# Earlier weight splits, an earlier statistics start and an earlier residual at the LayerNorm seams of a two-layer decoder kernel

## The chip, the cores and the metric

The kernel runs on one core of one Trainium2 chip. The metric is the device time of one execution in microseconds (us). The kernel before took 1182.99 us (median of 3 runs, 1182.77 to 1183.74).

The core's engines run side by side and meet at semaphores: PE is TensorE (matmuls), DVE is VectorE, ACT is ScalarE, POOL is GpSimd, SP issues the loads. Each engine takes its own instructions strictly in the order in which they are written; an instruction that waits holds up everything behind it on its engine.

## The reference

One step of a two-layer decoder over 512 prompt tokens and 32 sample tokens (8 sequences of 4), model width 1024, MLP width 4096, all in float32. What matters here is the shape of the chain:

```
for i in range(2):
    if i == 0:  m = recurrent_mixer(x, ...)        # Griffin block, ends in  (h * y) @ w_out + b_out
    else:       m = sliding_window_attention(x)    # x @ w_qkv ..., softmax with sink, @ w_o + b_o
    x = layer_norm(ALPHA * x + m, ln1_g[i], ln1_b[i])
    x = layer_norm(ALPHA * x + square(relu(x @ w_up[i])) @ w_down[i], ln2_g[i], ln2_b[i])

def layer_norm(x, g, b):
    mu = mean(x); var = mean(square(x - mu))
    return (x - mu) * rsqrt(var + 1e-5) * g + b
```

There are four LayerNorms, numbered L = 0 to 3 in the code: L = 0 and 2 follow a mixer's output projection, L = 1 and 3 follow an MLP. The whole token batch goes through all of them.

## The kernel before

**Layout.** The model dimension lies on the 128 partitions in eight tiles (k or m = 0 to 7), tokens lie on the free axis. The 544 tokens are two halves: h = 0 has 256, h = 1 has 288. `acc` holds the running sum, `x_hi` and `x_lo` the current activations.

**Two-part numbers.** Each float32 operand of a matmul is split in a high part (rounded) and a low part (the rest), and a product is three matmuls: hi\*hi, lo\*hi, hi\*lo. So each weight slab (128x1024) is loaded to one of 4 `stage` buffers, copied by ACT to `w_hi` (line 476) and subtracted by DVE to `w_lo` (line 797). This pair of operations is called a split of a slab. There are 8 slab slots; ACT's part of a split waits until the matmuls that last used the slot are done. The load of slab j waits for the DVE part of slab j-4.

**A seam.** Between a projection or MLP (PE) and the next one lies a LayerNorm, done half by half, so that the statistics of one half run beside the matmuls of the other. For each tile of the projection, DVE adds the PSUM bank to `acc` (line 969) and `acc` to a running sum (line 976): `add_tile`. ACT squares the tile (`square`, line 595; two `sqt` buffers, so the square of tile m waits for POOL's work on tile m-2), and POOL adds the squares up (`add_square`, line 1254). After tile 7, PE turns the two sums into a mean and a mean square for every partition with two matmuls against ones (`norm_sums`, lines 1375 and 1378); ACT copies the mean (603), DVE makes the variance (984 to 987), ACT takes the root (605), DVE subtracts the mean (1011), inverts the root (1014) and multiplies (1017), ACT writes `x_hi` and the scaled `acc` (616, 617; two tiles make a pair), DVE writes `x_lo` for the pair (1006, called the low step).

**Where norm_sums stands on PE.** For half 1 it stands inside the next group of matmuls (`group_by_half`, lines 1410 to 1412): after k = 1 in the first `up` group of an MLP, after k = 3 in the first q/k/v group. PE is in order, so the rest of the group is behind it.

**Work inside the seams.** The engines' idle places are filled by hand: `norm_apply` takes callbacks. In `tiles` (seams L = 0 and L = 2), `beside(t)` runs once for each pair t of half 0 and deals with the tiles of half 1 and with the first four slabs of the MLP (`late`). In `mlp`, the steps `up(l, 0)` to `up(l, 3)` (ACT: relu at 651, square at 653; DVE: square at 1053, low part at 1057) and the splits of slabs j0+4 to j0+7 (which the first `down` product reads, lines 1498 to 1500) lie between the LayerNorm's steps of half 1.

**POOL's residual.** For L = 1, POOL multiplies the normalised `acc` by ALPHA and adds the next bias (`residual`, line 1265), eight tiles a half; each waits for the low step of its pair. For l = 0 it stands behind all additions of squares of half 1.

The three places that the change touches are called seam A (L = 0 and the start of the first MLP, 170 to 215 us), seam C (L = 1, from the first MLP to q/k/v, 565 to 610 us) and seam E (L = 2 and the start of the second MLP, 757 to 802 us, the same code as A).

Of the kernel before, what the change touches and what calls it, by code (L numbers as in the profile page):

```python
# [73 lines left out]
def build(nc, xp_t, xs_t, vec, w_y, w_x, w_ga, w_gi, w_out, w_qkv, w_o, w_up, w_down,  # L74
          ck_t, cache_k, cache_v, y_t, small, k_p, v_p, k_s, v_s):
    ctx = ExitStack()
    with ctx:
# [374 lines left out]
        def _(act):  # L452
# [135 lines left out]
            def square(L, h, m):  # L588

                c0, n = HALF[h]  # L590
                pos = tile_pos(L, h, m)
                act.wait_ge(s_evV, read_by(unit_of("down" if L % 2 else "o", L, h, m) + 1, "V"))
                if pos >= 2:
                    act.wait_ge(s_s2, pos - 1)
                A(sqt[:, pos % 2, :n], acc[:, m, c0:c0 + n], ACT.Square).then_inc(s_sqt, 1)

            def norm_stats(L, h):
                _, n = HALF[h]
                m0 = mark[("ln", L, h)]
                idx = 2 * L + h  # L600
                if idx:
                    act.wait_ge(s_xhat, 4 * idx)
                A(mean[:, :n], unit(m0)[:, :n], ACT.Copy).then_inc(s_evA, 1)
                act.wait_ge(s_var, idx + 1)
                A(rstd[:, :n], msq[:, :n], ACT.Sqrt).then_inc(s_std, 1)
# [17 lines left out]
            def tiles(L, early, late):  # L623


                def beside(t):
                    if t:
                        square(L, 1, 2 + t)
                        split(late[t - 1:t])

                for m in range(KT):
                    split(early[m:m + 1])
                    square(L, 0, m)
                square(L, 1, 0)
                norm_stats(L, 0)
                square(L, 1, 1)
                square(L, 1, 2)
                norm_apply(L, 0, beside)
                square(L, 1, 6)
                square(L, 1, 7)  # L640
                split(late[3:])

            def up(l, q, c=0, i=0):

# [10 lines left out]
            def mlp(l):  # L655
                j0 = job_at[("mlp", l)][0]
                j7 = j0 + 8 * (CHUNKS - 1)
                L = 2 * l + 1
                norm_stats(2 * l, 1)
                split(range(j0 + 4, j0 + 6))  # L660
                up(l, 0)
                up(l, 1)
                split([j0 + 6])
                up(l, 2)
                split([j0 + 7])
                up(l, 3)
                norm_apply(2 * l, 1)
                for q in range(4, 8):
                    up(l, q)
                split(range(j0 + 8, j0 + 12))  # L670
                with act.Fori(0, CHUNKS - 2) as i:
                    for q in range(4):
                        for k in ((0, 1), (2,), (3,), ())[q]:
                            split([j0 + 12 + k], i, 8, 24, down_unit(l, 0, 1, 7) + 1)
                        up(l, q, 1, i)
                    for q in range(4, 8):
                        up(l, q, 1, i)

                    split(range(j0 + 16, j0 + 20), i, 8, 24, up_unit(l, 1, 1, 3) + 1)
                for q in range(4):  # L680
                    for k in ((0, 1), (2,), (3,), ())[q]:
                        split([j7 + 4 + k])
                    up(l, q, CHUNKS - 1)
                for m in range(KT):
                    square(L, 0, m)
                up(l, 4, CHUNKS - 1)
                norm_stats(L, 0)
                up(l, 5, CHUNKS - 1)
                up(l, 6, CHUNKS - 1)

                def beside(t):
                    if t == 1:
                        up(l, 7, CHUNKS - 1)
                    if t >= 2:
                        square(L, 1, 2 * t - 4)
                        square(L, 1, 2 * t - 3)

                norm_apply(L, 0, beside)
                gj = job_at[("qkv", 0)][0]
                for m in range(4, KT):  # L700
                    if l == 0:
                        split([gj + m - 4])
                    square(L, 1, m)

            tiles(0, (), next_slabs(("mlp", 0)))
            mlp(0)
# [75 lines left out]
        def _(dve):  # L782
# [240 lines left out]
            def add_tile(name, L, h, m):  # L1023
                n0 = unit_of(name, L, h, m)
                tile_done(L, h, m, unit(n0), read_by(n0 + 1, "V"))

            def tiles(name, L, early, late):


                def beside(t):  # L1030
                    add_tile(name, L, 1, 3 + t)
                    if t:
                        split(late[t - 1:t])

                for m in range(KT):
                    add_tile(name, L, 0, m)
                    if m % 2:
                        split(early[m // 2:m // 2 + 1])
                add_tile(name, L, 1, 0)
                norm_stats(L, 0)  # L1040
                norm_apply(L, 0, beside, after_centre=lambda: add_tile(name, L, 1, 1),
                           after_root=lambda: add_tile(name, L, 1, 2))
                add_tile(name, L, 1, 7)
                split(late[3:])

            def up(l, q, c=0, i=0):

# [25 lines left out]
            def mlp(l):  # L1073
                j0 = job_at[("mlp", l)][0]
                j7 = j0 + 8 * (CHUNKS - 1)
                L = 2 * l + 1
                norm_stats(2 * l, 1)

                def rest():
                    for q in range(1, 4):  # L1080
                        up(l, q)
                        if q > 1:
                            split([j0 + 4 + q])

                def sums(t):
                    if t == 1 or t == 2:
                        accumulate(l, 0, 0, 2 * t - 2)
                        accumulate(l, 0, 0, 2 * t - 1)

                norm_apply(2 * l, 1, sums, after_centre=lambda: (split([j0 + 4, j0 + 5]), up(l, 0)), after_root=rest)  # L1090
                for m in range(4, KT):
                    accumulate(l, 0, 0, m)
                for q in range(4, 8):
                    up(l, q)
                for m in range(KT):
                    if m < 4:
                        split([j0 + 8 + m])
                    accumulate(l, 0, 1, m)
                with dve.Fori(0, CHUNKS - 2) as i:
                    for q in range(4):  # L1100
                        for k in ((0, 1), (2,), (3,), ())[q]:
                            split([j0 + 12 + k], i, 8)
                        up(l, q, 1, i)
                    for m in range(KT):
                        accumulate(l, 1, 0, m, i)
                    for q in range(4, 8):
                        up(l, q, 1, i)
                    for m in range(KT):
                        if m < 4:
                            split([j0 + 16 + m], i, 8)  # L1110
                        accumulate(l, 1, 1, m, i)
                for q in range(4):
                    for k in ((0, 1), (2,), (3,), ())[q]:
                        split([j7 + 4 + k])
                    up(l, q, CHUNKS - 1)
                for m in range(KT):
                    add_tile("down", L, 0, m)
                up(l, 4, CHUNKS - 1)
                norm_stats(L, 0)
                gj = job_at[("qkv", 0)][0]  # L1120

                def ups(t):
                    if t == 0:
                        up(l, 6, CHUNKS - 1)

                def tail(t):
                    if t == 0:
                        up(l, 7, CHUNKS - 1)
                    if t == 1 or t == 2:
                        add_tile("down", L, 1, 2 * t - 2)  # L1130
                        add_tile("down", L, 1, 2 * t - 1)

                norm_apply(L, 0, tail, ups,
                           after_centre=lambda: up(l, 5, CHUNKS - 1))
                for m in range(4, KT):
                    add_tile("down", L, 1, m)
                    if l == 0:
                        split([gj + m - 4])

            dve.wait_ge(s_res0, 2)  # L1140
            tiles("o", 0, (), next_slabs(("mlp", 0)))
# [67 lines left out]
        def _(pool):  # L1209
# [65 lines left out]
            def mlp(l):  # L1275
                L = 2 * l + 1
                for m in range(KT):
                    add_square(L, 0, m)
                if l:
                    residual(L, 0)  # L1280
                for m in range(KT):
                    add_square(L, 1, m)
                if l == 0:
                    residual(L, 0)
                residual(L, 1)

            tiles(0)
# [461 lines left out]
```

## Time and profile before

| | |
|---|---|
| median of 3 runs | 1182.99 us |
| the profiled execution: own time | 1182.99 us |
| the profiled execution: span of the trace | 1181.2 us |
| PE busy | 1125.2 us (95%) |
| DVE busy | 686.8 us (58%) |
| ACT busy | 522.3 us (44%) |
| POOL busy | 166.1 us (14%) |
| mean granted clock of TensorE | 0.978 |

The page gives busy time by engine; the list of waits says for whom PE stood idle; the timeline gives every instruction with its start, its duration and, in square brackets, the idle time of its engine before it and what ended it. A row with x4 merges four instructions. Starts are counted from the beginning of the span.

### The profile page before, as it was taken

What the parts mean: (1) busy time and instruction counts of PE and PEld (TensorE: products, weight loads), DVE (VectorE), ACT (ScalarE), POOL (GpSimd) and SP (SyncE); (2) the same over time, 40 slices, a digit from 0 to 9 for tenths busy, and PEclk for the clock granted to TensorE, in tenths of its full rate; (3) what the DMA queues carried; (4) which work ended last, traced back from release to release, by engine and by line L of the source; (5) the groups of instructions that cost most, each with busy time, mean ns of one, the idle gap of its engine ahead of it and who ended that gap; (6) DMA issues with size and microseconds to landing.
All of it is one profiled execution on the core that took longest, in us unless ns stands there. A gap on an engine that the chain in (4) does not pass through costs nothing.

```text
span 1181.2 us, 23125 instructions
## 1 busy us (share of the span) xinstructions
PE 1125.2 (95%) x8783; PEld 1098.9 (93%) x8783; DVE 686.8 (58%) x1277; ACT 522.3 (44%) x1009; POOL 166.1 (14%) x205
## 2 busy tenths in 40 slices
PE   7899899999999999999999789999999999999994
PEld 7899899999999999999989458999999999999994
DVE  6888788545354463546942981685453543535566
ACT  5899836424232242233644991463242232422333
POOL 3212131000100000002530771210000000000024
PEclk9899899999999999999999898999999999999997
DMA  8222304133241230422311120042240422403202
GB/s 256 82 80 90 125 2 129 52 108 111 107 142 59 83 128 16 140 71 72 88 56 42 54 73 19 1 143 71 73 137 16 131 71 71 142 19 123 72 4 73
DMA packets 51468, 98.42 MB, mean 83 GB/s; under 512 B 4448, under 2 KB 20256, under 8 KB 51392
## 3 DMA queue, kind: packets, MB, share of 16 engines
q1 hardware_dynamic: 50720, 94.81, 25.2%
q0 software_dynamic: 400, 2.21, 0.5%
q8 instruction: 39, 0.64, 0.2%
q10 hardware_dynamic: 288, 0.59, 0.1%
q14 instruction: 21, 0.17, 0.0%
HBM read 95.06 MB, written 3.56 MB: 83 GB/s over the span
## 4 chain that ended last, share of the span: by engine, by line
PE 77%; DVE 10%; ACT 7%; issue 2%; POOL 2%; DMA 1%; SPq 0%; POOLq 0%; DVEq 0%; ACTq 0%
PE bank L1332 18%; PE bank L1333 18%; PE bank L1334 18%; PE bank L1500 5%; PE bank L1498 5%; PE bank L1499 5%; DVE w_lo L797 2%; PE bank L1410 1%; PE bank L1412 1%; PE bank L1411 1%; ACT w_hi L476 1%; POOL w_lo L1309 1%; DVE acc L1011 1%; DVE xc_odd L927 1%; PE bank L1580 1%
## 5 line engine op out<-in xcount | busy, mean ns | idle before, releaser
L1332 PE MATMUL bank<-x_hi,w_hi 128*128 128x288 f32 (+1 forms) x1360 | 397.2, 292 | 7.9 <-DVE w_lo L797 7.9
L1333 PE MATMUL bank<-x_lo,w_hi 128*128 128x288 f32 (+1 forms) x1360 | 395.3, 291 | 0.0
L1334 PE MATMUL bank<-x_hi,w_lo 128*128 128x288 f32 (+1 forms) x1360 | 393.2, 289 | 0.0
L1332 PEld LDWEIGHTS bank<-x_hi,w_hi 128*128 128x128 f32 x1360 | 259.2, 191 | 9.2 <-DVE w_lo L797 8.6
L1334 PEld LDWEIGHTS bank<-x_hi,w_lo 128*128 128x128 f32 x1360 | 259.7, 191 | 0.0
L1333 PEld LDWEIGHTS bank<-x_lo,w_hi 128*128 128x128 f32 x1360 | 259.4, 191 | 0.1
L797 DVE TENSOR_TENSOR w_lo<-stage,w_hi 128x1024 fp32r<-128x1024 f32 x162 | 198.1, 1236 | 45.5 <-ACT w_hi L476 45.5
L476 ACT ACTIVATE w_hi<-stage 128x1024 fp32r<-128x1024 f32 x170 | 172.3, 1049 | 117.2 <-PE bank L1334 112.3
L651 ACT ACTIVATE relu<-bank 128x256 f32<-128x256 f32 (+1 forms) x128 | 50.9, 398 | 352.4 <-PE bank L1334 329.1
L1333 PE MATMUL bank<-m_lo,w_hi 128*128 128x288 f32 (+1 forms) x608 | 176.0, 289 | 0.0
L1332 PE MATMUL bank<-m_hi,w_hi 128*128 128x288 f32 (+1 forms) x608 | 175.4, 289 | 0.0
L1334 PE MATMUL bank<-m_hi,w_lo 128*128 128x288 f32 (+1 forms) x608 | 175.2, 288 | 0.0
L1053 DVE TENSOR_TENSOR h_sq<-relu 128x256 f32<-128x256 f32 (+1 forms) x128 | 56.6, 442 | 172.0 <-ACT relu L651 172.0
L1070 DVE TENSOR_TENSOR acc<-bank,acc 128x256 f32<-128x256 f32 (+1 forms) x192 | 79.7, 439 | 129.8 <-PE bank L1334 65.5
L1498 PE MATMUL bank<-m_hi,w_hi 128*128 128x288 f32 (+1 forms) x512 | 148.1, 289 | 1.6 <-DVE w_lo L797 1.5
L1500 PE MATMUL bank<-m_hi,w_lo 128*128 128x288 f32 (+1 forms) x512 | 147.7, 288 | 0.0
L1499 PE MATMUL bank<-m_lo,w_hi 128*128 128x288 f32 (+1 forms) x512 | 147.4, 288 | 0.0
L1332 PEld LDWEIGHTS bank<-m_hi,w_hi 128*128 128x128 f32 x608 | 114.7, 189 | 0.0
L1333 PEld LDWEIGHTS bank<-m_lo,w_hi 128*128 128x128 f32 x608 | 114.5, 188 | 0.0
L1334 PEld LDWEIGHTS bank<-m_hi,w_lo 128*128 128x128 f32 x608 | 114.3, 188 | 0.0
L1498 PEld LDWEIGHTS bank<-m_hi,w_hi 128*128 128x128 f32 x512 | 96.5, 188 | 2.7 <-issue 2.2
L1499 PEld LDWEIGHTS bank<-m_lo,w_hi 128*128 128x128 f32 x512 | 96.5, 188 | 0.0
(188 smaller groups left out, 1522.2 us busy)
## 6 DMA issues: line engine op xcount, KB each, us to landing
stage<-w_up SPq DMA_DIRECT2D x64, 512.0 KB, 4.0
stage<-w_down SPq DMA_DIRECT2D x64, 512.0 KB, 3.6
stage<-w_qkv SPq DMA_DIRECT2D x10, 512.0 KB, 4.4
stage<-w_x SPq DMA_DIRECT2D x8, 512.0 KB, 5.0
stage<-w_y SPq DMA_DIRECT2D x8, 512.0 KB, 4.4
stage<-w_out SPq DMA_DIRECT2D x8, 512.0 KB, 4.1
stage<-w_o SPq DMA_DIRECT2D x8, 512.0 KB, 3.8
y_t<-acc SPq DMA_DIRECT2D x8, 144.0 KB, 1.9
```

Of the source, the lines that this page charges most:

```text
L476: A(hi, raw, ACT.Copy).then_inc(s_whi, 1)
L651: A(relu[:, q % 2, :n], bank[:, n0 % BANKS, :n], ACT.Relu).then_inc(s_evA, 1)
L797: vt.tensor_tensor(lo, raw, hi.bitcast(F32), ALU.subtract).then_inc(s_wlo, 1)
L927: ins = vt.scalar_tensor_tensor(xp, u[:, t, k:k + 256], wk, xp, ALU.mult, ALU.add)
L1053: vt.tensor_tensor(h_sq[:, q % 2, :n], relu[:, q % 2, :n], relu[:, q % 2, :n], ALU.mult)\
L1070: ins = vt.tensor_tensor(a, bank[:, n0 % BANKS, :n], a, ALU.add)
L1332: mm(out, wh, xh, start=(k == 0), stop=False)
L1333: mm(out, wh, xl, start=False, stop=False)
L1334: ins = mm(out, wl, xh, start=False, stop=(k == last))
L1498: mm(out, wh, xh, start=(k == 0), stop=False)
L1499: mm(out, wh, xl, start=False, stop=False)
L1500: ins = mm(out, wl, xh, start=False, stop=(k == 3))
```

## The change

Four edits, none of which changes what is computed.

1. In `tiles` (A, E): `beside(t)` deals with half 1's tile 3+t on both engines and splits slab `late[t]`. Before, ACT squared tile 2+t, neither engine split at t = 0, and the last slab came after tile 7.
2. At the start of `mlp` (A, E): the splits of slabs j0+4 and j0+5 move ahead of `norm_stats`, that of j0+6 to the place behind the centring, that of j0+7 between `up(l, 2)` and `up(l, 3)`; on DVE, `up(l, 2)` and `up(l, 3)` come after the first of the four multiplications.
3. At the end of the first MLP (C): the splits of the q/k/v slabs start at tile 6 instead of tile 4, so two of the four come after tile 7.
4. On POOL (C): `residual(1, 0)` goes ahead of half 1's additions of squares.

```
 ACT, tiles:    def beside(t):
-                    if t:
-                        square(L, 1, 2 + t)
-                        split(late[t - 1:t])
+                    square(L, 1, 3 + t)
+                    split(late[t:t + 1])
...
                 norm_apply(L, 0, beside)
-                square(L, 1, 6)
                 square(L, 1, 7)
-                split(late[3:])
 ACT, mlp:
+                split(range(j0 + 4, j0 + 6))
                 norm_stats(2 * l, 1)
-                split(range(j0 + 4, j0 + 6))
-                up(l, 0)
-                up(l, 1)
-                split([j0 + 6])
-                up(l, 2)
-                split([j0 + 7])
-                up(l, 3)
+                split(range(j0 + 6, j0 + 8))
+                for q in range(4):
+                    up(l, q)
...
                 for m in range(4, KT):
-                    if l == 0:
-                        split([gj + m - 4])
+                    if l == 0 and m >= 6:
+                        split([gj + m - 6])
                     square(L, 1, m)
+                if l == 0:
+                    split([gj + 2, gj + 3])
 DVE, tiles:
                     add_tile(name, L, 1, 3 + t)
-                    if t:
-                        split(late[t - 1:t])
+                    split(late[t:t + 1])
...
-                norm_apply(2 * l, 1, sums, after_centre=lambda: (split([j0 + 4, j0 + 5]), up(l, 0)), after_root=rest)
+                norm_apply(2 * l, 1, sums, ups, after_centre=lambda: (split([j0 + 6]), up(l, 0)),
+                           after_root=lambda: up(l, 1))
...
 POOL, mlp:
-                if l:
-                    residual(L, 0)
+                residual(L, 0)
                 for m in range(KT):
                     add_square(L, 1, m)
-                if l == 0:
-                    residual(L, 0)
                 residual(L, 1)
```

**ACT in seam A, before,** from pair 0 of half 0 (four rows of 616 and 617) to the square of tile 3 and the end of pair 1. Line numbers are those of the kernel named.

```order
L616 ACTIVATE x_hi<-acc,vecs 128x256
L617 ACTIVATE acc<-acc,vecs 128x256
L616 ACTIVATE x_hi<-acc,vecs 128x256
L617 ACTIVATE acc<-acc,vecs 128x256
L616 ACTIVATE x_hi<-acc,vecs 128x256
L617 ACTIVATE acc<-acc,vecs 128x256
L616 ACTIVATE x_hi<-acc,vecs 128x256
L617 ACTIVATE acc<-acc,vecs 128x256
L595 ACTIVATE sqt<-acc 128x288
L476 ACTIVATE w_hi<-stage 128x1024
```

The same place in the changed kernel:

```order
L616 ACTIVATE x_hi<-acc,vecs 128x256
L617 ACTIVATE acc<-acc,vecs 128x256
L616 ACTIVATE x_hi<-acc,vecs 128x256
L617 ACTIVATE acc<-acc,vecs 128x256
L595 ACTIVATE sqt<-acc 128x288
L476 ACTIVATE w_hi<-stage 128x1024
L616 ACTIVATE x_hi<-acc,vecs 128x256
L617 ACTIVATE acc<-acc,vecs 128x256
L616 ACTIVATE x_hi<-acc,vecs 128x256
L617 ACTIVATE acc<-acc,vecs 128x256
```

The square of tile 3 and the first slab's copy now stand after pair 0 instead of after pair 1.

**DVE in seam A, before,** at pairs 0 and 1 of half 0: the low step (1006), then the two additions of one tile of half 1 (969, 976), then from pair 1 on a slab's low part (797).

```order
L1006 TENSOR_TENSOR x_lo<-acc,x_hi 128x2x256
L969 TENSOR_TENSOR acc<-bank,acc 128x288
L976 TENSOR_TENSOR sum_b<-acc,sum_b 128x288
L1006 TENSOR_TENSOR x_lo<-acc,x_hi 128x2x256
L969 TENSOR_TENSOR acc<-bank,acc 128x288
L976 TENSOR_TENSOR sum_b<-acc,sum_b 128x288
L797 TENSOR_TENSOR w_lo<-stage,w_hi 128x1024
```

The same place in the changed kernel:

```order
L1002 TENSOR_TENSOR x_lo<-acc,x_hi 128x2x256
L965 TENSOR_TENSOR acc<-bank,acc 128x288
L972 TENSOR_TENSOR sum_b<-acc,sum_b 128x288
L793 TENSOR_TENSOR w_lo<-stage,w_hi 128x1024
L1002 TENSOR_TENSOR x_lo<-acc,x_hi 128x2x256
L965 TENSOR_TENSOR acc<-bank,acc 128x288
L972 TENSOR_TENSOR sum_b<-acc,sum_b 128x288
L793 TENSOR_TENSOR w_lo<-stage,w_hi 128x1024
```

On DVE the additions keep their place behind the low step; only a slab's low part is added at pair 0.

**POOL in seam C,** before: the additions of squares of half 0 (`sumsq_a`) and half 1 (`sumsq_b`), then the residual of half 0 (128x256) and half 1.

```order
L1254 TENSOR_TENSOR sumsq_a<-sqt,zeros 128x256
L1254 TENSOR_TENSOR sumsq_a<-sqt,sumsq_a 128x256 x7
L1254 TENSOR_TENSOR sumsq_b<-sqt,zeros 128x288
L1254 TENSOR_TENSOR sumsq_b<-sqt,sumsq_b 128x288 x7
L1265 TENSOR_SCALAR acc<-acc,vecs 128x256 x8
L1265 TENSOR_SCALAR acc<-acc,vecs 128x288 x8
```

And in the changed kernel:

```order
L1252 TENSOR_TENSOR sumsq_a<-sqt,zeros 128x256
L1252 TENSOR_TENSOR sumsq_a<-sqt,sumsq_a 128x256 x7
L1263 TENSOR_SCALAR acc<-acc,vecs 128x256 x8
L1252 TENSOR_TENSOR sumsq_b<-sqt,zeros 128x288
L1252 TENSOR_TENSOR sumsq_b<-sqt,sumsq_b 128x288 x7
L1263 TENSOR_SCALAR acc<-acc,vecs 128x288 x8
```

The eight residual steps of half 0, each of which waits for a low step, now stand ahead of every addition of half 1's squares.

## Rows read from the trace of the kernel before

**Rows 1.** List of waits of PE: line, whom it waited for, us in total, times, longest.

```profile
PE bank L1410 <- DVE acc L1068: 2.7, 2, 1.4
```

**Rows 2.** Timeline of PE, seams A and E: start, duration, line, operation, idle before.

```profile
189.35 0.65 PE L1375 MATMUL bank<-sum_b,ones 128*128 128x288 f32 x2
189.83 0.65 PE L1378 MATMUL bank<-sumsq_b,ones 128*128 128x288 f32 x2
...
204.64 0.36 PE L1498 MATMUL bank<-m_hi,w_hi 128*128 128x256 f32 x1 [0.34 <-DVE w_lo L797]
...
213.33 0.37 PE L1410 MATMUL bank<-x_hi,w_hi 128*128 128x288 f32 x1 [1.37 <-DVE acc L1068]
...
776.27 0.65 PE L1375 MATMUL bank<-sum_b,ones 128*128 128x288 f32 x2
```

**Rows 3.** Timeline of ACT, seam A: squares, slab copies and a pair's first write.

```profile
176.85 0.43 ACT L595 ACTIVATE sqt<-acc 128x288 f32<-128x288 f32 x1
177.18 1.04 ACT L476 ACTIVATE w_hi<-stage 128x1024 fp32r<-128x1024 f32 x1
178.13 0.59 ACT L616 ACTIVATE x_hi<-acc,vecs 128x256 fp32r<-128x256 f32 x1
...
180.10 0.43 ACT L595 ACTIVATE sqt<-acc 128x288 f32<-128x288 f32 x1
```

**Rows 4.** Timeline of DVE, seam A: low steps, additions, statistics, a hidden low part, multiplications.

```profile
175.80 0.45 DVE L969 TENSOR_TENSOR acc<-bank,acc 128x288 f32<-128x288 f32 x1
176.28 0.46 DVE L976 TENSOR_TENSOR sum_b<-acc,sum_b 128x288 f32<-128x288 f32 x1
...
180.30 0.69 DVE L1006 TENSOR_TENSOR x_lo<-acc,x_hi 128x512 fp32r<-128x512 f32 x1 [0.43 <-ACT acc L617]
...
190.54 0.46 DVE L984 TENSOR_TENSOR msq<-mean 128x288 f32<-128x288 f32 x1 [0.70 <-ACT mean L603]
...
202.94 0.43 DVE L1057 TENSOR_TENSOR m_lo<-h_sq,m_hi 128x256 fp32r<-128x256 f32 x1
...
204.41 2.76 DVE L1017 TENSOR_TENSOR acc<-acc,rstd 128x576 f32<-128x576 f32 x4
```

**Rows 5.** Timeline of POOL: seam A's last addition, seam C's residuals of both halves.

```profile
187.70 0.82 POOL L1254 TENSOR_TENSOR sumsq_b<-sqt,sumsq_b 128x288 f32<-128x288 f32 x1 [0.67 <-ACT sqt L595]
...
585.95 10.12 POOL L1265 TENSOR_SCALAR acc<-acc,vecs 128x256 f32<-128x256 f32 x8
601.10 0.99 POOL L1265 TENSOR_SCALAR acc<-acc,vecs 128x288 f32<-128x288 f32 x2 [5.03 <-DVE x_lo L1006]
```

**Rows 6.** Timeline of ACT, seam C: the first q/k/v slab and the fifth.

```profile
575.29 1.04 ACT L476 ACTIVATE w_hi<-stage 128x1024 fp32r<-128x1024 f32 x1
...
585.14 1.06 ACT L476 ACTIVATE w_hi<-stage 128x1024 fp32r<-128x1024 f32 x1 [0.17 <-DMA stage<-w_qkv]
```

**Rows 7.** Timeline of DVE, seam C: the last low step, the first slab, statistics, two slabs.

```profile
575.65 1.30 DVE L1006 TENSOR_TENSOR x_lo<-acc,x_hi 128x512 fp32r<-128x512 f32 x1
...
577.73 1.22 DVE L797 TENSOR_TENSOR w_lo<-stage,w_hi 128x1024 fp32r<-128x1024 f32 x1
...
588.10 0.65 DVE L984 TENSOR_TENSOR msq<-mean 128x288 f32<-128x288 f32 x1
...
592.71 2.55 DVE L797 TENSOR_TENSOR w_lo<-stage,w_hi 128x1024 fp32r<-128x1024 f32 x2
```

**Rows 8.** Timeline of PE, seam C: starts of the three q/k/v groups.

```profile
579.68 0.35 PE L1410 MATMUL bank<-x_hi,w_hi 128*128 128x256 f32 x1 [1.80 <-DVE acc L969]
...
595.31 0.39 PE L1332 MATMUL bank<-x_hi,w_hi 128*128 128x256 f32 x1 [2.84 <-DVE w_lo L797]
...
608.33 0.29 PE L1410 MATMUL bank<-x_hi,w_hi 128*128 128x288 f32 x1
```

**Rows 9.** Loads of the page: operation, count, size, us to landing.

```profile
stage<-w_qkv SPq DMA_DIRECT2D x10, 512.0 KB, 4.4
```

**Rows 10.** Stretches: busy us of PE, PEld, DVE, ACT, POOL, granted clock, DMA, GB/s.

```profile
596.00:598.00 2.00, 2.00 (x11) 2.00 (x11) 1.97 (x3) 0.05 (x1) 0.07 (x1) 0.50 0.89 286
```

More of the change, by code:

```diff
@@ L1043, in tiles @@
                 add_tile(name, L, 1, 7)
-                split(late[3:])
             def up(l, q, c=0, i=0):
@@ L1076, in mlp, with ups @@
                 L = 2 * l + 1
+                split(range(j0 + 4, j0 + 6))
                 norm_stats(2 * l, 1)
[L1079 to L1083, printed above, removed]
+                def ups(t):
+                    if t == 0:
+                        up(l, 2)
+                        split([j0 + 7])
+                        up(l, 3)
                 def sums(t):
@@ L1135, in mlp @@
                 for m in range(4, KT):
+                    if l == 0 and m >= 6:
+                        split([gj + m - 6])
                     add_tile("down", L, 1, m)
-                    if l == 0:
-                        split([gj + m - 4])
+                if l == 0:
+                    split([gj + 2, gj + 3])
             dve.wait_ge(s_res0, 2)
@@ L1278, in mlp @@
                     add_square(L, 0, m)
-                if l:
-                    residual(L, 0)
+                residual(L, 0)
                 for m in range(KT):
                     add_square(L, 1, m)
-                if l == 0:
-                    residual(L, 0)
                 residual(L, 1)
```

## The prediction

> **What bounds the kernel now.** PE is busy for 1125 of 1181 us, so the time is PE's matmuls plus the places where PE stands. The list of waits comes first: away from the beginning and the attention part it shows three stops at the LayerNorm seams. Twice 1.4 us before an `up` group that waits for DVE to free its banks [rows 1], once 1.80 and once 2.84 us in seam C [rows 8]. The timeline of PE says what stands ahead of each stop. In seams A and E the statistics matmuls run at 189.35 and 776.27 without a wait [rows 2]; the two seams are the same code, 586.92 us apart, so I work out A and count it twice. Outside the seams PE never stands between 214 and 549 us, nor in the second MLP, so a delay of PE at the end of a seam is carried in full to the end of the kernel. The timelines of ACT, DVE and POOL then say which engine feeds the statistics, and how much room it has.
>
> **Edit 1, seams A and E: the pairs of half 0.** Before, ACT's step for one pair is: four writes, one square, one slab copy. Squares start at 176.85 and 180.10, a period of 3.25 us [rows 3]: ACT's own work, with no idle time, because the tile that ACT squares after pair t was added by DVE after pair t-1. Now ACT squares tile 3+t right behind pair t, and DVE adds that tile only behind its low step of the same pair, which in turn waits for ACT's last write of that pair. So one step is a serial chain over both engines:
>
> - pair's first write to DVE's low step: 178.13 to 180.30, 2.17 us [rows 3, 4]
> - low step to addition: 180.30 to 180.91, 0.61; the addition itself 0.45 [rows 4]
> - square to slab copy 0.33, slab copy to the next pair's first write 0.95 [rows 3]
>
> Sum 4.51 us, against 3.25. The first tile's addition (tile 3) stands at 175.80, done 176.25 [rows 4], so pair 1 starts at 176.25 + 0.33 + 0.95 = 177.53, pair 2 at 182.04, pair 3 at 186.55. Tile 6 is added at 186.55 + 2.78 = 189.33; the last slab's copy runs from 190.11 to 191.15; DVE's low part of it (1.22 us by the row in seam C [rows 7], 1.14 to the next start) until 192.3; only then tile 7 is added, until 192.75, squared by 193.2, and POOL's 0.82 us [rows 5] ends at 194.1. The second statistics matmul, which PE issued at 189.83 [rows 2], can start at about 194.2. PE is in order, so it stands from 189.35 to 194.2 but for one matmul: a new stop of 4.4 us beyond the old time. The banks don't bring it forward: the tiles that the `up` group overwrites are added by about 185.4.
>
> **Edit 2, seams A and E: the start of the MLP.** After square 7 ACT copies slabs j0+4 and j0+5 (193.1 to 195.1; their loads have landed, since their buffers come free earlier than before), DVE makes their low parts until 196.4, and the variance starts there: 5.9 us later than 190.54 [rows 4]. From here the new order is better. Before, the low part of `up(l, 3)` was done at 203.37, 12.83 us after the variance's start [rows 4]. Of the three slab parts that lay between, two are left (-1.14), and one multiplication is added (2.76 / 4 = +0.69 [rows 4]): 12.4 us, so 208.8. PE's `down` product needs that part for k = 3; from its k = 3 to the end of the product PE took from 204.64 to 213.33 - 1.37 = 211.96, 7.32 us [rows 2], or 0.122 a matmul for 60. The product so ends at 216.2. The 1.37 us stop for the banks goes: the first multiplication is done early, so ACT writes pair 0 while DVE is still in the `up` steps, and the four banks are free at about 215.5, which is 0.7 us too early to count. Net for A: 216.2 - 213.33 = +2.9 us.
>
> To this comes the clock. With the full clock PE would have 1.5 us to spare before 208.9 (194.4 + 72 x 0.12 + 36 x 0.12 = 207.4). The stop of 2.84 us before 595.31 [rows 8] was followed by a granted clock of 0.50 [rows 10], the 1.2 GHz level, and the q/k/v group behind it took 608.33 - 595.31 = 13.02 us for 96 matmuls, 1.5 us more than 96 x 0.12. One such spell fits in the spare 1.5 us and costs nothing; two cost about 1.7. Bounds for A: +1.2 (DVE never late, PE's own work alone: 194.4 + 168 x 0.12 = 214.6) and +4.6 (two spells). I take +3.4, near the chain with a little of the clock; E the same.
>
> The Trainium skill, "TensorE: Matmul & The Clock Gate", Part 1, says that an array left idle falls to half rate and must be busy again before it is let up. By that rule each new stop of almost 5 us surely brings a slow spell; by the row alone it is likely. The rule would move each of A and E towards its upper bound.
>
> **Edits 3 and 4, seam C.** ACT's square of tile m waits for POOL's addition of tile m-2. Before, POOL was idle there. Now eight residual steps stand ahead of its first addition, and the last two wait for the low step of pair 3, which ended at 576.95 [rows 7]. A residual step costs 0.50 us alone and 10.12 / 8 = 1.27 beside a busy DVE [rows 5], so POOL reaches tile 0 at about 578 and ends it at 579. ACT's square of tile 2 waits for it, and squares 3, 4, 5 follow at POOL's pace, 0.85 to 0.9 each: 582. Edit 3 has put the first q/k/v slab behind square 5; its copy began at 575.29 [rows 6], now at about 582.1. With 1.04 for the copy and 1.22 for the low part PE can start q/k/v at 584.4 instead of 579.68 [rows 8]: +4.7 us. Bounds: 583.3 with every POOL step at its undisturbed price, 586.5 with every one at 1.27 or more.
>
> Then the next slabs are late too. DVE is done with the second one at about 586.4 (tile 6 stands between), its buffer's load takes 4.4 us [rows 9], and copy and low part 2.3: 593.2. The variance starts there instead of at 588.10 [rows 7]. Its steps and the centring took 592.71 - 588.10 = 4.6 us beside POOL's residuals; these are gone, so 4.0. Two slabs more, 2.4 instead of 2.55 [rows 7]: the group at 595.31 starts at 599.6, +4.3. PE will by then have finished the group before at about 599, so it hardly stands a second time, and the 1.5 us of slow clock behind 595.31 are not paid here. Group q/k/v of half 1 starts at 599.6 + 11.5 = 611.1 instead of 608.33 [rows 8]: +2.8. I take +2.7. Bounds: +0.5 (undisturbed POOL, no slow spell) and +6 (two slow spells, loads at twice the wait).
>
> The Trainium skill, "SBUF — State Buffer", "Who interferes with whom", says that a DVE instruction with two SBUF inputs and a GpSimd instruction that reads SBUF block each other. The rows agree (0.50 against 1.27). This rule speaks for edit 4, but what it could give back is the 0.6 us that I took at the variance.
>
> **Sum.** 3.4 + 2.7 + 3.4 = 9.5 us. The profiled execution took 1182.99 us (span 1181.2 and 1.8 around it), which is the median of the runs too. Forecast 1192.5.
>
> **Rivals.**
>
> 1. Two slow spells of the clock at each new stop. For it: three stops of about 5 to 6 us each. Against: in A and E a part lies under DVE's chain. Price: A and E 4.6, C 5.0: 1197.2. Chance 0.17.
> 2. Seam C costs next to nothing: POOL catches up and the second stop's slow spell is saved. For it: POOL's low price alone [rows 5]. Price: C +0.5, A and E at the chain's 2.9: 1189.3. Chance 0.18.
> 3. Not slower: tile 7's sums reach PE by about 189.8, the stop never arises, and the bank stop (1.37) and the stop of 0.34 ahead of 204.64 [rows 2] go. From the start of pair 1 the chain needs two steps and 7.5 us, so this needs a step of 2.4 us or less where 4.5 is worked out; it could only be if DVE didn't queue the additions behind the low steps. Price: 2 x -1.7, C 0: 1179.6. Chance 0.04.
> 4. The change trades evenly: shorter chains after the variance give back what the stops take. PE's own work sets +1.2 in A as a floor, so this needs seam C to gain 2.4. 1183.0, chance 0.03.
>
> **How the numbers follow.** My own case has 0.58. Changes under 0.2% (2.4 us) can't be told from none. Range 1187.5 to 1197.5: it covers rivals 1 and 2 and both bounds but the outermost. Faster 0.04, same 0.03, slower 0.93.
>
> **What would show it.** In the changed profile PE waits for `sum_b` or `sumsq_b` at the statistics matmuls of A and E, 4 to 5 us each; ACT's squares in A stand 4.5 us apart and wait for DVE's addition; the two bank waits are gone; in C ACT's square of tile 2 waits for POOL, and the first q/k/v group waits 6 to 7 us for a slab's low part. If squares in A stay 3.25 apart, or no wait stands at the statistics matmuls, I am wrong.

## The result and the profile after

The changed kernel takes 1191.23 us (median of 4 runs, 1190.14 to 1192.63), against 1182.88 us for the kernel before in the same comparison: ratio 1.0073, 95% interval 1.0055 to 1.0090. It is slower by about 8.5 us. The profiled execution has a span of 1188.6 us (1181.2 before); about 1 us of the difference to the medians is that this execution reached seam A 0.95 us earlier, at 185.54 instead of 186.49. The lead is there before anything that the edits moved: the first write of pair 0, at 171.94 instead of 172.89, is as much earlier. Across all runs below that start lies between 185.5 and 187.4. So I compare stretches, from PE's first matmul of one group to that of another, and not only whole times.

From the list of waits of PE in the changed kernel (line, whom it waited for, us in total, times, longest):

```profile
PE bank L1370 <- DVE sum_b L972: 9.1, 3, 4.0
...
PE bank L1327 <- DVE w_lo L793: 6.3, 4, 3.3
PE bank L1405 <- DVE w_lo L793: 5.2, 1, 5.2
```

The two bank waits of [rows 1] are gone. In their place stand two waits of 4.0 us at the statistics matmuls (the third, of 1.0, stands at the end of the kernel in both) and one of 5.2 at the first q/k/v group. The timeline of PE in seams A and E, to be read against [rows 2]:

```profile
192.56 1.33 PE L1370 MATMUL bank<-sum_b,ones 128*128 128x288 f32 x2 [4.01 <-DVE sum_b L972]
193.69 1.17 PE L1373 MATMUL bank<-sumsq_b,ones 128*128 128x288 f32 x2
194.24 0.83 PE L1405 MATMUL bank<-x_hi,w_hi 128*128 128x256 f32 x1
...
204.66 0.28 PE L1493 MATMUL bank<-m_hi,w_hi 128*128 128x256 f32 x1
...
216.07 0.29 PE L1405 MATMUL bank<-x_hi,w_hi 128*128 128x288 f32 x1
...
784.96 1.33 PE L1370 MATMUL bank<-sum_b,ones 128*128 128x288 f32 x2 [4.01 <-DVE sum_b L972]
```

The pairs of half 0 on ACT ([rows 3] before). Each square now waits 1.2 to 1.3 us for DVE's addition of the same tile:

```profile
175.32 0.45 ACT L595 ACTIVATE sqt<-acc 128x288 f32<-128x288 f32 x1 [1.30 <-DVE acc L965]
175.67 1.05 ACT L476 ACTIVATE w_hi<-stage 128x1024 fp32r<-128x1024 f32 x1
176.62 0.58 ACT L616 ACTIVATE x_hi<-acc,vecs 128x256 fp32r<-128x256 f32 x1
...
179.88 0.45 ACT L595 ACTIVATE sqt<-acc 128x288 f32<-128x288 f32 x1 [1.20 <-DVE acc L965]
```

And on DVE ([rows 4] before), where the addition follows the low step, which waits for ACT's last write; then the variance and the end of `up(l, 3)`:

```profile
178.79 0.69 DVE L1002 TENSOR_TENSOR x_lo<-acc,x_hi 128x512 fp32r<-128x512 f32 x1 [0.81 <-ACT acc L617]
179.40 0.45 DVE L965 TENSOR_TENSOR acc<-bank,acc 128x288 f32<-128x288 f32 x1
...
195.75 0.45 DVE L980 TENSOR_TENSOR msq<-mean 128x288 f32<-128x288 f32 x1
...
207.90 0.42 DVE L1051 TENSOR_TENSOR m_lo<-h_sq,m_hi 128x256 fp32r<-128x256 f32 x1
```

Seam C, the starts of the three q/k/v groups on PE ([rows 8] before):

```profile
585.79 0.55 PE L1405 MATMUL bank<-x_hi,w_hi 128*128 128x256 f32 x1 [5.24 <-DVE w_lo L793]
...
601.25 0.39 PE L1327 MATMUL bank<-x_hi,w_hi 128*128 128x256 f32 x1 [0.83 <-DVE w_lo L793]
...
612.75 0.29 PE L1405 MATMUL bank<-x_hi,w_hi 128*128 128x288 f32 x1
```

The stretches of all runs, in us. A and E run from the first `up` matmul of half 0 to the first `up` matmul of half 1. C runs from the start of the last `down` product of half 1; the three columns are the starts of the first q/k/v group, the second, and the first one of half 1. The medians come from several comparisons, in which the kernel before had 1182.18 to 1183.06; each ratio is to the kernel before of its own comparison and isn't simply the quotient of the medians shown.

| run | A | E | C: first | C: second | C: half 1 | median | ratio and interval |
|---|---|---|---|---|---|---|---|
| before | 26.84 | 26.83 | 14.72 | 30.35 | 43.37 | 1182.88 (with the changed kernel) | |
| changed | 30.53 | 29.81 | 18.16 | 33.62 | 45.12 | 1191.23 | 1.0073 (1.0055 to 1.0090) |
| ae_only (edits 1, 2) | 30.49 | 29.89 | 14.73 | 30.34 | 41.86 | 1187.67 | 1.0052 (1.0037 to 1.0066) |
| c_only (edits 3, 4) | 26.86 | 26.87 | 18.17 | 33.98 | 45.50 | 1183.70 | 1.0012 (1.0003 to 1.0021) |
| edit1_only | 32.24 | 31.68 | 14.73 | 30.34 | 43.31 | 1192.59 | 1.0088 (1.0074 to 1.0102) |
| edit2_only | 25.17 | 25.16 | 14.72 | 30.34 | 41.86 | 1177.28 | 0.9960 (0.9947 to 0.9974) |
| square_lag | 24.89 | 24.90 | 14.72 | 30.34 | 41.85 | 1177.32 | 0.9960 (0.9946 to 0.9974) |
| add_ahead | 25.35 | 25.69 | 14.72 | 30.36 | 43.40 | 1178.64 | 0.9966 (0.9954 to 0.9978) |
| edit3_only | 26.85 | 26.87 | 16.16 | 32.97 | 45.91 | 1185.70 | 1.0029 (1.0018 to 1.0040) |
| edit4_only | 26.86 | 26.87 | 16.76 | 31.55 | 43.07 | 1181.69 | 0.9996 (0.9987 to 1.0005) |
| edit3_add_first | 26.84 | 26.84 | 16.37 | 31.66 | 43.07 | 1182.87 | 1.0001 (0.9991 to 1.0011) |
| residual_last | 26.85 | 26.84 | 14.72 | 29.42 | 42.38 | 1180.46 | 0.9983 (0.9974 to 0.9992) |
| edit2_residual_last | 25.16 | 25.17 | 14.73 | 29.50 | 41.02 | 1177.23 | 0.9954 (0.9940 to 0.9968) |
| lag_residual_last | 24.91 | 24.90 | 14.72 | 29.52 | 41.03 | 1175.62 | 0.9940 (0.9926 to 0.9953) |

The changed kernel's span follows from its row: A +3.69, C +1.75, E +2.98, and -0.95 ahead of A make +7.5; the spans differ by 7.4. The stretches between the seams agree with before to 0.1 us.

### The profile page after: what moved, and what is told of

The parts are those of the page before. It is cut to its first block, busy times and chain, and to the rows that moved or that the text cites. A ratio compares the mean times of both kernels' runs of the same rounds, so it can differ in the third digit from the quotient of the medians.

```text
span 1188.6 us, 23125 instructions
## 1 busy us (share of the span) xinstructions
PE 1128.6 (95%) x8783; PEld 1101.3 (93%) x8783; DVE 683.7 (58%) x1277; ACT 522.7 (44%) x1009; POOL 153.3 (13%) x205
## 4 chain that ended last, share of the span: by engine, by line
PE 80%; DVE 8%; ACT 6%; POOL 2%; issue 2%; DMA 1%; SPq 0%; POOLq 0%; DVEq 0%; ACTq 0%
PE bank L1327 18%; PE bank L1328 18%; PE bank L1329 18%; PE bank L1493 5%; PE bank L1495 5%; PE bank L1494 5%; ACT w_hi L476 2%; PE bank L1405 2%; PE bank L1407 2%; PE bank L1406 2%; DVE w_lo L793 1%; POOL w_lo L1304 1%; PE bank L1575 1%; DMA stage<-w_y 1%; DVE xc_odd L923 1%
```

## The experiments

Theory: the seams A and E are slower because ACT and DVE now wait for each other in every pair; PE stands at the statistics matmuls; edit 2 gives a part back. Rivals: ACT's earlier slab copies are too much work in that place, or edit 2's slabs ahead of the statistics are the harm.

**Which seam.** ae_only keeps edits 1 and 2, c_only keeps edits 3 and 4.

> Edits 1 and 2 alone (seams A and E), seam C as before. Theory (serial chain of ACT and DVE in the pairs of half 0, PE then stands at the statistics matmuls): A +3.7 and E +3.0 us as in the changed kernel, so 1189.5 (ratio 1.0057), with two waits of 4.0 us of PE for sum_b. Rival (the slab parts moved into seam C's neighbourhood matter, A and E only shift): under +3 us.

> Edits 3 and 4 alone (seam C), seams A and E as before. Theory: POOL's residual ahead of the additions of squares holds ACT's squares and with them the first q/k/v slab; PE waits 5.2 us for it, the second wait shrinks from 2.8 to 0.8: +1.8 us, 1184.7 (ratio 1.0015). Rival (C carries the cost of a slow clock in either case and so costs as much as A): +3.5 us or more.

The stretches of A, E and C's two first groups agree with the changed kernel within 0.4 us in both, so the seams don't act on each other but for the clock. Both whole times came out below what the stretches would make them. The span of ae_only's profiled execution is 4.4 us longer than before's (1185.6 and 1181.2), where A and E cost 6.7; 1.5 us of the difference lie in seam C, whose half 1 starts at 41.86 instead of 43.37 by the place of a slow clock (see the last section), and 0.7 ahead of A (185.82 instead of 186.49). c_only's C costs 2.13 and its ratio is 1.0012; in its profiled execution the attention part, between C and E, took 163.5 us where it took 165.1 before, with the same program.

**Serial chain, or too much work.** square_lag changes only which tile ACT squares:

```
 ACT, tiles (on top of edits 1 and 2):
                 def beside(t):
-                    square(L, 1, 3 + t)
+                    square(L, 1, 2 + t)
                     split(late[t:t + 1])
...
-                square(L, 1, 2)
                 norm_apply(L, 0, beside)
+                square(L, 1, 6)
                 square(L, 1, 7)
```

> Edits 1 and 2, but ACT squares the tile that DVE added one pair earlier (2+t beside pair t, tiles 6 and 7 behind), slabs split as in the changed kernel; seam C as before. Theory (only the serial chain costs, the earlier slabs and the new order of the MLP's start pay): squares 3.25 us apart, no wait at the statistics matmuls, variance starts 0.8 us later than before at most, PE is let into the next up group 2 us earlier in A and in E: 1179.0 (ratio 0.9966). Rival (ACT's extra slab copy among the pairs is itself too much work in that place): still a wait for sum_b or sumsq_b of 1 us or more, and 1184 to 1187.

Measured 0.9960 (0.9946 to 0.9974), an improvement where the changed kernel loses. ACT's squares in seam A of this run:

```profile
178.19 0.43 ACT L595 ACTIVATE sqt<-acc 128x288 f32<-128x288 f32 x1
181.44 0.43 ACT L595 ACTIVATE sqt<-acc 128x288 f32<-128x288 f32 x1
```

They are 3.25 us apart and wait for nobody, with the same four slab copies among the pairs as in the changed kernel. So the copies are not the harm. Of the 5.7 us by which its span is shorter than before's (1175.5 and 1181.2), the stretches of A and E hold 3.9; 1.5 more come from seam C (41.85 instead of 43.37), where nothing was changed. add_ahead is the test from the other side: ACT's program in A and E is word for word that of the changed kernel (seam C is as before), and DVE adds one tile ahead.

```
 DVE, tiles (on top of edits 1 and 2):
+                def ahead(t):
+                    if t == 3:
+                        add_tile(name, L, 1, 3)
                 def beside(t):
-                    add_tile(name, L, 1, 3 + t)
+                    if t < 3:
+                        add_tile(name, L, 1, 4 + t)
                     split(late[t:t + 1])
-                norm_apply(L, 0, beside, after_centre=...
+                norm_apply(L, 0, beside, ahead, after_centre=...
```

> As edits 1 and 2 of the changed kernel, ACT's program unchanged (it squares tile 3+t beside pair t), but DVE adds each tile one pair ahead of it: tile 3 behind the multiplications, tile 4+t behind low step t. Theory (the chain is closed by the place of DVE's addition): ACT's squares are again about 3.25 us apart, the wait at the statistics matmuls falls from 4.0 us to under 0.5, A takes about 25.5 us from the first up group to the second (26.84 before, 30.5 in the changed kernel): 1179 to 1181. Rival (ACT's own extra copy at pair 0 makes it late): squares stay over 4 us apart and A stays over 29.

```profile
179.36 0.43 ACT L595 ACTIVATE sqt<-acc 128x288 f32<-128x288 f32 x1
182.61 0.43 ACT L595 ACTIVATE sqt<-acc 128x288 f32<-128x288 f32 x1
...
188.91 0.45 ACT L595 ACTIVATE sqt<-acc 128x288 f32<-128x288 f32 x1 [1.66 <-DVE acc L963]
```

Again 3.25 us, no wait stands at the statistics matmuls, and A takes 25.35. Moving either end of the hand-off by one tile opens the chain. That is shown from both sides.

**What edit 2 does.** Edit 1 and edit 2, each alone.

> Edit 1 alone, the start of the MLP in its old order. Theory: the wait of 4.0 us at the statistics matmuls is as in the changed kernel, and the old order gives nothing back behind it: A and E +4.2 each, 1191.3 (ratio 1.007). Rival (edit 2 has a part in the stop, since its slab copies stand ahead of the statistics): the wait is under 3 us and the time under 1188.

> Edit 2 alone: the pairs of half 0 as before, the start of the MLP in the new order. Theory (edit 2 pays by itself, since DVE's last up step and the freeing of the banks come earlier): no wait at the statistics matmuls, the bank wait of 1.4 us gone twice, variance 1.5 us later but 12.4 instead of 12.8 us to the last up part: 1.4 us gained in A and E each, 1180.2 (ratio 0.9976). Rival (its gain exists only behind the stop of edit 1, because there PE is late anyway): 1183, ratio 1.000.

Edit 1 alone costs 5.40 in A and 4.85 in E, more than I expected (4.2); with edit 2 the two cost 3.69 and 2.98. Edit 2 alone gains 1.67 in each, and so stands for 1.7 to 1.9 in either setting: it doesn't need the stop of edit 1. Its rival has fallen. Most of it is the stop for the banks: PE waits 1.35 us (A) and 1.34 us (E) for them in edit1_only as it did before, and in edit2_only this wait is gone. The span of edit2_only, 6.0 us shorter than before's, again holds the 1.5 us of seam C beside the 3.3 us of the two stretches. square_lag adds only 0.28 and 0.26 us a seam to edit 2, so nearly all that was to be had at the start of the MLP came from edit 2, and the earlier slabs of edit 1 were worth a quarter of a microsecond. In its whole time the gain can't be told from edit 2's (1177.32 and 1177.28).

**Seam C.** Edits 3 and 4, each alone.

> Edit 3 alone: the q/k/v slabs' splits start at tile 6, POOL as before. Theory (loads and low parts of the fifth and sixth slab come later, so the variance starts 1.7 us later): the first q/k/v group starts 0.4 us later, the second 1.7 us later, 1184.5 (ratio 1.0013). Rival (POOL's residual is the whole cost of seam C): 1183.0 (1.000).

> Edit 4 alone: POOL's residual of half 0 ahead of the additions of half 1's squares, splits from tile 4 on as before. Theory: ACT's square of tile 2 waits about 3 us for POOL as with both edits, but the first slab is split right behind square 3: the first q/k/v group starts 1.2 us later, the second 1.2 us later, 1184.2 (ratio 1.001). Rival (edit 3 is the whole cost): 1183.0 and the first group on time.

For the first q/k/v group the two edits add up: 1.44 + 2.04 = 3.48, measured together 3.44. At the second group edit 3 costs 2.62 (expected 1.7), edit 4 costs 1.20 (expected 1.2), and both together 3.27 to 3.63. At the start of half 1's group edit 3 costs 2.54, edit 4 alone is 0.30 us faster than before, and both together cost 1.75 to 2.13. The step from +1.20 to -0.30 is the clock and not POOL: before, the group behind the second stop took 13.02 us, partly at a granted clock of 0.50 [rows 8, 10]. In edit4_only the second stop was 0.70 us, the granted clock behind it 1.00, and the group took 607.74 - 596.22 = 11.52:

```profile
596.22 0.39 PE L1329 MATMUL bank<-x_hi,w_hi 128*128 128x256 f32 x1 [0.70 <-DVE w_lo L797]
...
607.74 0.29 PE L1407 MATMUL bank<-x_hi,w_hi 128*128 128x288 f32 x1
```

Against ae_only, where seam C is as before and the clock behind the second stop is 1.00 too, edit 4 costs 43.07 - 41.86 = 1.21 us. So its whole time can't be told from before's (0.9996) because of the clock: behind its first stop of 3.84 us the granted clock was 0.50 inside the first group (582 to 584), where PE was going to wait for DVE anyway, and 1.00 behind the second stop. Whether all its executions go so is not shown. From the first group (+2.04) to the second (+1.20) edit 4 does give something back, and the timelines show where. ACT's square waits 3.08 us for POOL as expected:

```profile
576.89 0.45 ACT L595 ACTIVATE sqt<-acc 128x288 f32<-128x288 f32 x1 [3.08 <-POOL sumsq_b L1254]
```

but POOL is free when the statistics come, and DVE's steps there run undisturbed ([rows 7] before):

```profile
589.92 0.46 DVE L984 TENSOR_TENSOR msq<-mean 128x288 f32<-128x288 f32 x1
...
593.81 2.35 DVE L797 TENSOR_TENSOR w_lo<-stage,w_hi 128x1024 fp32r<-128x1024 f32 x2
```

From the variance to the two slabs' low parts is 593.81 - 589.92 = 3.89 us, where it was 592.71 - 588.10 = 4.61. That is the 0.6 us that the prediction took here, measured as 0.7.

Edit 3 also turns DVE's order round: a slab's low part now stands ahead of the tile's addition. edit3_add_first undoes that alone:

```
 DVE, mlp (on top of edit 3):
                 for m in range(4, KT):
+                    add_tile("down", L, 1, m)
                     if l == 0 and m >= 6:
                         split([gj + m - 6])
-                    add_tile("down", L, 1, m)
```

> Edit 3 alone with DVE's order of before inside it: DVE adds tile 6 (7) and then makes the low part of the slab, instead of the other way round. Theory (edit 3 costs by the late start of the first slab, +1.4 us on the first q/k/v group, and by a second serial chain: copy, low part, addition, square, next copy, 3.05 us a slab): the first group starts 1.4 us later as with edit 3, but the second group comes about 2 us earlier than with edit 3 alone, about 31 us after the last down group's start (30.35 before, 32.97 with edit 3). Rival (the late loads of the fifth and sixth slab set it): the second group stays at 32.5 or more.

The second group comes at 31.66 instead of 32.97: the hand-off within edit 3 was worth 1.3 us, not 2. (Half 1's group, at 43.07, is 0.3 us ahead of before's, again because the group behind the second stop ran at the full clock, 11.41 us.) The timelines of ACT show both halves of the answer. With edit 3 alone a square waits 1.66 us for DVE's addition, which waits for the low part, which waits for ACT's copy, and squares 6 and 7 stand 3.05 us apart:

```profile
580.45 0.45 ACT L595 ACTIVATE sqt<-acc 128x288 f32<-128x288 f32 x1 [1.66 <-DVE acc L971]
583.50 0.45 ACT L595 ACTIVATE sqt<-acc 128x288 f32<-128x288 f32 x1 [1.66 <-DVE acc L971]
```

With the order turned back they stand 1.97 apart (580.24 and 582.21), and the fifth and the sixth slab's copies wait for their loads instead:

```profile
582.21 0.45 ACT L595 ACTIVATE sqt<-acc 128x288 f32<-128x288 f32 x1 [0.60 <-DVE acc L971]
...
585.42 1.06 ACT L476 ACTIVATE w_hi<-stage 128x1024 fp32r<-128x1024 f32 x1 [0.86 <-DMA stage<-w_qkv]
587.76 1.06 ACT L476 ACTIVATE w_hi<-stage 128x1024 fp32r<-128x1024 f32 x1 [1.28 <-DMA stage<-w_qkv]
```

So theory and rival each hold half: of edit 3's 2.62 us at the second group 1.3 are the serial hand-off. The other 1.3 are what is left, and I put them to the late start of the slabs and their loads; no run moved the loads alone.

**Where the residual can go.** On top of the kernel before, nothing but POOL's order changes.

```
 POOL, mlp:
-                if l == 0:
-                    residual(L, 0)
                 residual(L, 1)
+                if l == 0:
+                    residual(L, 0)
```

> The kernel before with one edit: for L = 1 POOL does the residual of half 1 first and that of half 0 last (the next reader of both is the attention's output projection). Theory (the 10.1 us of residual beside DVE slow DVE's low parts, variance and centring): with POOL idle there the second q/k/v group starts about 1 us earlier than 595.3, its stop shrinks from 2.8 to 1.9 and may bring no slow clock: 1180.5 to 1182 (ratio 0.998 to 0.999). Rival (DVE doesn't lose, only POOL does): 1183.0.

Ratio 0.9983 (0.9974 to 0.9992). With POOL idle there, DVE's steps from the variance to the two slabs' low parts took 591.45 - 587.58 = 3.87 us instead of 4.61, so the rival has fallen: DVE did lose beside the residual. The second group starts 0.93 us earlier and its stop is 1.9 us; the slow clock behind it stayed. In the whole time more was gained (about 2 us). In the profiled execution the rest lies in the attention part, which took 163.2 us here and 165.1 before; its granted clock falls in other places, which I take for the cause, but no run shows it alone. POOL's new order isn't it: edit2_residual_last has the same order and took 165.1 there, c_only has not and took 163.5.

**The combinations.** The residual's new place on top of edit 2 alone, and on top of edits 1 and 2 with the lagging square.

> Edit 2 and the residual of half 0 last. If their gains add: A and E 25.2 us each (-1.7 each), the second q/k/v group at 29.4 (-0.9), and less than 1 us more or less by where a slow clock falls: 1177.5 to 1178.5 (ratio 0.996). If seam C's gain was the slow clock alone, already saved in edit 2's run: 1178.5 to 1179.

> The version the experiments point to: edit 2, slabs split one pair earlier with ACT's squares one tile behind, residual of half 0 last. Gains that add: A and E -1.95 each, C -0.9 and the slow clock of 1.5 us behind the second q/k/v group: 1176 to 1177.5 (ratio 0.995). If the gains don't add: no better than 1177.3.

By stretches the gains add: A and E -1.67 or -1.93 each, second q/k/v group -0.85, half 1's group -2.34. Of these 2.34, 1.5 are the place of the slow clock, which edit2_only and square_lag had already gained (41.86 and 41.85) without a change in seam C; the residual's own part is 0.83 us. By whole times edit2_residual_last (1177.23) can't be told from edit2_only; its profiled execution also reached seam A 1.4 us later than edit2_only's. lag_residual_last is the fastest by its median: 1175.62 us, ratio 0.9940 (0.9926 to 0.9953), 7 us faster than the kernel before and 15.6 us faster than the changed one. Its interval overlaps with that of the others near 0.996, so its lead over them is likely and not shown. Its profiled execution also had the short attention part (163.5 us), where edit2_residual_last, with the same order on POOL, had 165.1.

## Why the prediction was right

The forecast was 1192.5 us, range 1187.5 to 1197.5; measured 1191.2. By seams, forecast 3.4 + 2.7 + 3.4 = 9.5 us, measured 3.69 + 1.75 + 2.98 = 8.4. The mechanism of A and E is the one forecast. That their sum was met to 0.1 us is in part luck, since one lies above the forecast and the other below. Of the signs that the prediction named all came but for one size: the first q/k/v group waited 5.24 us, not 6 to 7. Step by step:

**The pair's step.** Worked out 4.51 us, measured 4.56 (175.32 to 179.88). The chain has the links that the prediction named, and both of its ends, moved by one tile, open it (square_lag, add_ahead).

**The stop at the statistics.** Forecast: the group resumes 7.9 us after its first matmul (194.4 against 186.49); measured 8.70 (185.54 to 194.24). The sums came as forecast, within 0.3 us on before's clock (the last addition of squares ended at 193.36); the difference is that the statistics matmuls themselves ran at a slow clock, 1.33 us for the first two records instead of 0.65.

**From the variance on.** The variance started 5.9 us later by the forecast; measured 195.75 against 190.54 - 0.95, 6.16. From there to the end of `up(l, 3)` forecast 12.4, measured 12.57. The bank wait went, as forecast.

**The clock.** The prediction had one slow spell as free and two as 1.7 us more than the chain's 2.9. The granted clock of the changed kernel in seams A (first four stretches) and E, in the columns of [rows 10]:

```profile
192.00:194.00 2.00, 1.44 (x3) 1.09 (x4) 1.00 (x3) 1.95 (x3) 0.79 (x1) 0.50 0.56 162
194.00:196.00 2.00, 2.00 (x9) 1.71 (x9) 2.00 (x3) 0.68 (x2) 0.00 (x0) 0.50 0.35 108
196.00:198.00 2.00, 2.00 (x12) 2.00 (x11) 1.93 (x5) 0.93 (x2) 0.00 (x0) 0.53 0.87 265
198.00:200.00 2.00, 2.00 (x19) 2.00 (x18) 2.00 (x4) 1.42 (x2) 0.00 (x0) 1.00 0.73 249
...
786.00:788.00 2.00, 2.00 (x8) 1.72 (x8) 2.00 (x2) 1.08 (x2) 0.00 (x0) 0.50 0.48 190
788.00:790.00 2.00, 2.00 (x17) 2.00 (x17) 1.93 (x5) 0.53 (x2) 0.00 (x0) 0.90 0.75 210
```

The half level (1.2 GHz) lasted until about 198 in A and 788 in E, that is about 5.4 and 3.2 us of PE's work behind the stop: long in A, short in E. So A cost 3.69 and E 2.98, where 3.4 was taken for each. In A PE itself became the last: its `down` product began at 204.66 and needed 11.4 us with no stop to 216.07; `up(l, 3)` was done at 208.3, before PE's k = 3 at about 208.9. In E the two met: `up(l, 3)` was done at 800.5, and PE's k = 3 began at 800.55. So E cost what the chain over DVE gives (2.9), and the 0.7 us more in A are the clock's.

**Seam C: the term that was mis-sized.** Forecast +4.7 us for the first group, +4.3 for the second, +2.7 taken for the whole; measured +3.44, +3.27, +1.75. The step that was off is "the last two wait for the low step of pair 3, which ended at 576.95". That low step and the one of pair 2 took 1.30 us each before, beside POOL's additions of squares, and two of DVE's additions there took 0.78; with POOL waiting in the changed kernel the low steps took 0.69 and the additions 0.46 to 0.48:

```profile
577.06 0.69 DVE L1002 TENSOR_TENSOR x_lo<-acc,x_hi 128x512 fp32r<-128x512 f32 x1
```

It ended at 577.75, which is 575.1 on before's clock (C began 2.67 us later): 1.9 us earlier, 0.61 from each low step and 0.6 from the two additions. Behind it POOL's last two residual steps and its first addition took about what the forecast had for them. ACT's copy of the first slab began at 583.03, 580.4 on before's clock, where I had 582.1. From the copy to PE's start it took 2.76 us where I had 2.26, which gives 0.5 back. I used the rows for POOL's steps and forgot DVE's own steps beside POOL. The Trainium skill, "SBUF — State Buffer", "Who interferes with whom", says that a DVE instruction with two SBUF inputs contends with a GpSimd instruction that reads SBUF. The trace agrees (1.30 against 0.69).

The forecast also had no term for the hand-off inside edit 3. It let the second slab's low part end 2.0 us after the first one's (584.4 and 586.4); measured 3.05 (585.54 and 588.59), the step at which the squares of edit3_only stand apart. At the second group DVE's earlier steps outweigh this: +3.27 where I had +4.3. Taken alone, edit 4 costs more than edit 3 at the first group (2.04 and 1.44) and less at the second (1.20 and 2.62), where half of edit 3's cost is the hand-off that the prediction did not see there.

**The second stop's slow clock in C.** As forecast, the second stop shrank (0.83 us) and the group behind it ran at the full clock (612.75 - 601.25 = 11.50 us against 13.02 before).

## What to carry to other kernels

When work is moved between two in-order engines, write out for each step who hands over to whom: if engine 1 does item t only after engine 2's item t, and engine 2's item t stands behind something that waits for engine 1's same step, the two alternate and the period is the sum; one item of lag on either side restores the larger of the two. Look at the moved work's place relative to its neighbour on both engines, since that was worth 1.3 us in seam C and 5.6 and 4.9 us in A and E (the changed kernel against square_lag), and the earlier slabs themselves a quarter of a microsecond. And a step's duration read beside a busy neighbour is not its duration once the neighbour is moved: the low step of 1.30 us took 0.69.

## What was not expected of the hardware

A slow spell of TensorE's clock costs or not by where it falls. Seam C has the same program in the kernel before and in ae_only, and its two groups start at 14.7 and 30.3 us in both; yet half 1's group starts at 43.37 before and at 41.86 in ae_only. Before, the clock fell to 0.50 behind the second stop [rows 10]. In ae_only it stayed at 1.00 there:

```profile
596.00:598.00 2.00, 0.67 (x6) 0.47 (x4) 2.00 (x2) 0.57 (x2) 2.00 (x2) 1.00 0.12 19
598.00:600.00 2.00, 1.79 (x15) 1.79 (x16) 2.00 (x2) 0.00 (x0) 0.97 (x2) 1.00 0.69 253
```

and the second stop was shorter, 1.55 us instead of 2.84 [rows 8], because a slow spell fell inside the group ahead of it (granted clock low from 583.7 to 587.1) and this group ended later, while the slab for which PE waits came at the same time:

```profile
598.21 0.39 PE L1326 MATMUL bank<-x_hi,w_hi 128*128 128x256 f32 x1 [1.55 <-DVE w_lo L791]
```

In all fourteen profiled executions the start of half 1's group goes by this stop. Behind a second stop of 1.55 us or less it came 11.4 to 11.5 us after the second group (nine executions, edit4_only and the changed kernel among them); behind one of 1.9 us (residual_last) or of 2.8 us (before, edit1_only, add_ahead, edit3_only) it came 12.9 to 13.0 us after it. The five runs that differ from the kernel before only in A and E fall on both sides: ae_only, edit2_only and square_lag on the first, edit1_only and add_ahead on the second. So it isn't shown that a change elsewhere moves the spell; it may differ from execution to execution of one kernel, whose times range from 1180.3 to 1184.1 for the kernel before.

This is 1.5 us, 0.13% of the kernel, and the attention part moves by up to 1.9 us (163.2 to 165.2) between runs, with the granted clock falling in other places. So for a change of one or two microseconds the stretch says what was done, and the whole time says it plus the clock's place. Which way a spell falls was not made to order in any run, and stays open.
